# A two-layer hybrid decoder step: the queries' projection beside the selection bits, x kept in DRAM meanwhile, conditioning steps regrouped

## The chip, the cores and the metric

The kernel runs on one NeuronCore of a Trainium2 chip. TensorE (PE) multiplies matrices into PSUM, VectorE (DVE), ScalarE (ACT) and GpSimd (POOL) work elementwise, and SyncE (SP) issues nearly all of the DMAs, one after the other in the order in which they are written. Each engine has its own instruction stream, and semaphores connect the streams. The metric is the device time of one execution in microseconds, lower is better.

## The reference, cut to what matters

One inference step for 1024 new prompt rows and 8 samples of 4 new rows each (1056 rows in all, width 1024). Layer 0 is attention in which an indexer chooses the keys; layer 1 pools over windows; each is followed by an MLP. Every layer is conditioned on a vector c by shifts, scales and gates.

```python
for i in range(DEPTH):                                  # 2 layers
    mod = silu(c) @ w_mod[i] + b_mod[i]                 # 1024 -> 6*1024: the conditioning
    sh1, sc1, g1, sh2, sc2, g2 = jnp.split(mod, 6, axis=-1)
    h = modulate(rmsnorm(x, norm_mix_g[i]), sh1, sc1)
    m = dsa_mixer(h) if i == 0 else pool_mixer(h)
    x = x + g1[:, None, :] * m
    h = modulate(rmsnorm(x, norm_ffn_g[i]), sh2, sc2)
    x = x + g2[:, None, :] * (jnp.square(relu(h @ w_up[i])) @ w_down[i])

# dsa_mixer, layer 0
q, k, v, qi, ki, wi = jnp.split(h @ w_in, PROJ_SPLITS, axis=-1)   # 1024, 256, 256, 512, 64, 8 columns
logits = jnp.einsum('nqhd,nsd->nqhs', qi, kidx) * IDX_DIM ** -0.5
score = jnp.einsum('nqhs,nqh->nqs', relu(logits), wi) * IDX_HEADS ** -0.5
_, idx = lax.top_k(where(causal, score, -inf), k_sel)   # the best 256 (samples: 129) keys of each row
o = softmax attention of q over the chosen k, v         # 8 heads, 2 key heads
return o.reshape(n, t, -1) @ w_o
```

The samples' past keys, values and indexer keys lie in pages of 128 rows, found through page_table.

## The kernel before, in words

Everything is written by hand, engine by engine, in blocks; at the end of a block all engines meet at a barrier. x lies transposed in SBUF for the whole run (128 partitions, 8 chunks of 1056 columns). All large products are made in three parts: weights and rows are split into an upper and a lower half (hhi, hlo for the rows; whi, wlo for the weights), and `products` (L501) runs 24 matmuls of 352 columns for one unit of 128 output columns and a third of the rows. A *unit* of weights comes in three steps: SP loads it (`load_unit`, L463, 512 KB, which waits until the unit before the last has been split), ACT makes whi (`split_unit_hi`, L473), POOL makes wlo (`split_unit_lo`, L479). There are two slots, so the next unit can be made ready while PE multiplies with this one.

A *conditioning step* is 256 of the columns of w_mod: a load of 1 MB (L408), a product with the conditioning vector (`mod_product`, L424, 8 matmuls), a copy of the result by DVE, a fold by PE (`mod_turns`, L433) and an addition of the bias by DVE (`mod_bias`, L439). There are 48; they are placed wherever PE has time.

The blocks that matter here, in order:

- **Load and first norm** (0 to 50 us): x comes in and is transposed, 8 conditioning steps.
- **Projection** (L923, 50 to 263 us): 17 units. Units 0 and 1 give v, 2 and 3 k, 4 to 11 the queries q, 12 the indexer's key and weights, 13 to 16 the indexer's queries. SP's stream holds nothing but the unit loads.
- **Indexer** (L1045, 263 to 369 us): logits and scores, 8 conditioning steps, and the zeroed and regrouped queries of the samples, `qps` (L1250).
- **Selection** (L1305, 369 to 525 us): the threshold of the 256th best score is found bit by bit, in 31 bits. In each, ACT counts four of the seven score tiles against the candidate (L1382) and DVE three (L1445), and DVE sets the bit. Beside the bits run 30 conditioning steps, and the samples' past keys are loaded page by page (`load_kpg`, L395, and `load_pages`, L390), transposed on PE (L1339), copied and multiplied with `qps` (L1352).
- **Samples' attention** (L1533), **prompt attention** (L1676), **output projection** (L1817, x is added to here for the first time, L523), then the MLPs and layer 1.

The page loads need a page number from SBUF each, so SP reads a register before every one:

```python
def load_pages(sp, dst, cache, signal, b):                       # L390
    for n in range(PAGES):
        sp.dma_start(dst[:, n, :], cache[0, bass.ds(page(sp, b, n), 1)]...)
```

Of the kernel before, what the change touches and what calls it, by code (L numbers as in the profile page):

```python
# [16 lines left out]
NB = 8  # L17
# [51 lines left out]
U_KIWI = 12  # L69
# [73 lines left out]
def hybrid_step(nc, x_prompt, x_sample, cache_k, cache_v, cache_kidx, state_pool, page_table, c_prompt, c_sample,  # L143
# [3 lines left out]
    with ctx:  # L147
# [95 lines left out]
        put = region(r1)  # L243
        score = put("score", [P, P * sum(t + 1 for t in IDX_TILES)])
        scs = put("scs", [NS, SL])
        qps = put("qps", [P, NB, KV, HEADS * DT])
        ptb = put("ptb", [1, NB * PAGES], I32)
        tie = put("tie", [P, SEQ])
        tie_run = put("tie_run", [P, SEQ])
        ssm = put("ssm", [P, 2, SL])  # L250
        kpg = put("kpg", [P, 2, PAGES, KW])

        kir = put("kir", [P, 2, PAGES, ID])
# [3 lines left out]
        wsel = put("wsel", [P, 2, NS])  # L257
        qis = put("qis", [ID, NB, IH * DT])
        qit = put("qit", [ID, IH // 2, NS])


        moved = put("moved", [P, 2, IH // 2, P], F32R)
        assert moved.manual_sbuf_range[1] <= s1
# [3 lines left out]
        ki_hi = at("ki_hi", [P, SEQ], F32R, tie.manual_sbuf_range[0])  # L267
        ki_lo = at("ki_lo", [P, SEQ], F32R, tie_run.manual_sbuf_range[0])

        put = region(kpg.manual_sbuf_range[1])  # L270
        kts = put("kts", [P, 2, KV, PAST])
        junk_a = at("junk_a", [P, SEQ], F32, tie.manual_sbuf_range[0])
        junk_v = at("junk_v", [P, SEQ], F32, tie_run.manual_sbuf_range[0])

        mraw1 = [at(f"mraw1_{i}", [P, KT8, 256], F32, t.manual_sbuf_range[0]) for i, t in enumerate((wraw, whi, wlo))]

# [4 lines left out]
        assert kts.manual_sbuf_range[1] <= pts.manual_sbuf_range[1]  # L281

        vpg2 = put("vpg2", [P, 2, PAGES, KW])
        mrow1 = put("mrow1", [P, 2, 256])
        srows = put("srows", [P, 2, KW])
        assert srows.manual_sbuf_range[1] <= s1

        vpg6 = at("vpg6", [P, NB - 2, PAGES, KW], F32, qi.manual_sbuf_range[0])
        assert vpg6.manual_sbuf_range[1] <= wi.manual_sbuf_range[1]
        vpg = [vpg2[:, b] for b in range(2)] + [vpg6[:, b] for b in range(NB - 2)]  # L290

        put = region(ssm.manual_sbuf_range[0])
# [54 lines left out]
        mraw1_in = [sem(f"mraw1_in{i}") for i in range(3)]  # L347
# [63 lines left out]
        M_INDEX, M_SELECT = 8, 30  # L411
        M_REST = 2 * MOD_STEPS - M_FIRST - M_INDEX - M_SELECT

        MOD_SLOT = [n % 2 for n in range(M_INDEX)] + [n % 3 for n in range(M_SELECT + M_REST)]

        def load_mod1(sp, n):

            load_mod_step(sp, M_FIRST + n, mraw1[MOD_SLOT[n]][:, :, :], mraw1_in[MOD_SLOT[n]])

        def mod1_landed(pe, n):  # L420
            pe.wait_ge(mraw1_in[MOD_SLOT[n]], 16 * MOD_SLOT[:n + 1].count(MOD_SLOT[n]))
            return mraw1[MOD_SLOT[n]]
# [363 lines left out]

        NH = M_FIRST
# [134 lines left out]

        with nc.Block() as block:  # L923
            @block.sync
            def _(sp):
                for u in range(2, N_IN):
                    cols = u_in_cols(u)
                    load_unit(sp, u, raw8(u % 2)[:, :, 0:cols.stop - cols.start],
                              dsa_w_in[0, :, cols].rearrange("(k p) c -> p k c", p=P))

# [12 lines left out]
            def _(act):  # L943
# [16 lines left out]

                norm_root(act, 0)
# [5 lines left out]
                for s in range(6):  # L967
                    part(4 + s)
                    rows_of_v(s)
                for u in range(10, N_IN):  # L970
                    part(u)

            @block.gpsimd
            def _(pool):
                for u in range(N_IN):
                    split_unit_lo(pool, u, u % 2)

            @block.tensor
            def _(pe):
# [19 lines left out]
                for u in range(2, N_IN):  # L999
# [8 lines left out]
                    if 3 <= u < 9:  # L1008
                        rows_of_v(u - 3)

            @block.vector
            def _(dve):
# [5 lines left out]
                for u in range(2, N_IN):  # L1018
                    dst = u_in_dst(u, kt, qt, qi)
                    for c in range(NC):  # L1020
# [9 lines left out]
                        ins.then_inc(down_empty, 1)  # L1030

# [11 lines left out]
        assert len(logit_list) == 10 * M_INDEX and 24 < M_SELECT <= BITS and 2 <= M_REST <= 3  # L1043
        last_logit = {t: max(n for n, l in enumerate(logit_list) if l[0] == t) for t in IDX_TILES}
        with nc.Block() as block:  # L1045
            @block.sync
            def _(sp):
# [12 lines left out]
                load_mod1(sp, 0)  # L1060
# [11 lines left out]
                load_mod1(sp, 1)  # L1072
# [4 lines left out]
                loads += [(10 * n - 11, "step", n) for n in range(2, M_INDEX + 2)]  # L1077
                for _, kind, n in sorted(loads):
                    if kind == "pages":
                        load_kir(n)  # L1080
                        if n < 4:
                            load_kpg(sp, n - 2)
                    else:
                        sp.wait_ge(mod_mm, M_FIRST + n - 1)
                        load_mod1(sp, n)
# [13 lines left out]
            def _(pe):  # L1099
# [34 lines left out]
                def mod_half(m, half):  # L1134

                    if half == 0 and m >= 2:
                        pe.wait_ge(mod_done, M_FIRST + m - 1)
                    weights = mod1_landed(pe, m)
                    mod_product(pe, bank(MOD_BANK[m % 2]), weights, range(4 * half, 4 * half + 4))

                def mod_turn(m):
                    pe.wait_ge(mod_row, M_FIRST + m + 1)
# [23 lines left out]
                pe.wait_ge(mod_done, M_FIRST + M_INDEX)  # L1166
# [5 lines left out]
                for a, (lo, hi) in enumerate(((0, PAST), (PAST, SL))):  # L1172
                    for g in range(2):
                        ins = pe.matmul(pair[3][0:NS, a, 0:hi - lo], wsel[:, g, :], ssm[:, g, lo:hi], start=(g == 0),
# [4 lines left out]
            def _(act):  # L1179
# [37 lines left out]
                for g in range(2):  # L1217
                    act.activation(ssm[:, g, 0:PAST], bank(2 + 2 * g), ACT.Relu, scale=SC_IDX)
                    act.activation(ssm[:, g, PAST:SL], bank(3)[:, DT * g:DT * (g + 1)], ACT.Relu,
# [3 lines left out]
            def _(dve):  # L1223
# [26 lines left out]
                dve.memset(qps[:], 0.0).then_inc(qprep, 1)  # L1250
                dve.wait_ge(qprep, 9)
                for g in range(KV):
                    for r in range(GROUP):
                        h = GROUP * g + r
                        ins = dve.tensor_copy(qps[:, :, g, h * DT:(h + 1) * DT],
                                              qt[:, h, SEQ:ROWS].rearrange("p (b t) -> p b t", t=DT))
                    ins.then_inc(qprep, 1)
                dve.wait_ge(krow_wi, TILES)
                for n, (t, h, c) in enumerate(logit_list):
# [12 lines left out]
                    if n % 10 == 9:  # L1272
# [4 lines left out]
                        else:  # L1277
                            dve.wait_ge(mod_t, M_FIRST + m)
                        dve.wait_ge(mod_mm, M_FIRST + m + 1)
                        dve.tensor_copy(krow[:, 0, 0:256],  # L1280
                                        bank(MOD_BANK[m % 2])[:, 0:256]).then_inc(mod_row, 1)
                    if n % 10 == 5 and n > 10:
                        mod_bias(dve, M_FIRST + n // 10 - 1, bank(MOD_BANK[(n // 10 - 1) % 2])[:, 256:512])
# [6 lines left out]
                mod_bias(dve, M_FIRST + M_INDEX - 1, bank(MOD_BANK[(M_INDEX - 1) % 2])[:, 256:512])  # L1290
# [13 lines left out]
        m1 = M_FIRST + M_INDEX  # L1304
        with nc.Block() as block:  # L1305
            @block.sync
            def _(sp):
                load_mod1(sp, M_INDEX + 2)
                for n in range(3, M_SELECT):
                    sp.wait_ge(mod_mm, m1 + n - 2)  # L1310
                    load_mod1(sp, M_INDEX + n)
                    if n % 3 == 0 and n // 3 + 1 < NB:
                        b = n // 3 + 1
                        if b >= 2:
                            sp.wait_ge(kts_t, 2 * b - 2)
                            load_kpg(sp, b)
                    if n % 3 == 1 and n // 3 < NB:
                        load_pages(sp, vpg[n // 3], cache_v, vpg_in[n // 3], n // 3)
                load_pages(sp, vpg[0], cache_v, vpg_in[0], 0)
                for n in range(M_SELECT, M_SELECT + M_REST):  # L1320
                    sp.wait_ge(mod_mm, m1 + n - 2)
                    load_mod1(sp, M_INDEX + n)
# [7 lines left out]

# [1071 lines left out]
```

## Time and profile before

| | us |
|---|---|
| median of 3 runs | 2475.91 (2474.41 to 2481.66) |
| the profiled execution | 2483.4 |
| its span, first to last instruction | 2481.6 |
| PE busy | 2291.1 (92%) |
| DVE busy | 997.4 (40%) |
| ACT busy | 782.4 (32%) |
| mean granted TensorE clock | 0.952 |

PE is busy nearly everywhere. In forty equal slices of 62 us its busy share is `6999886768888999...`, and the granted clock, in tenths of full speed, is `8999886769999999...`: the slices that are not full are the first and those from about 250 to 560 us, which hold the indexer, the selection and the samples' attention. The DMA engines move 310 GB/s in the slice of 434 to 496 us and 35 to 57 GB/s in the projection. A busy time is summed over an engine's instructions; a wait names what released it. In a timeline row the first number is the start in us, the second the extent of the row from its first to its last instruction, and what stands in brackets is the idle time before it.

### The profile page before, as it was taken

To read this page: it belongs to the slowest core of one execution; us is meant where nothing else is said; L and a number is where in the kernel's file an instruction comes from. 1 tells how busy PE (TensorE), PEld (TensorE's weight loads), DVE (VectorE), ACT (ScalarE), POOL (GpSimd) and SP (SyncE) were. 2 spreads that over 40 slices of the span, in tenths; PEclk is the share of its full clock that TensorE was granted. 3 is DMA by queue.
4 is the path that set the end of the run, shared out by engine and by line. 5 is a ranking of instruction groups with operands and counts; after the bars stand their busy time and mean duration, and the time that the engine had idled before them with its cause. 6 is when DMAs were issued, how large, how long until landed. Compare 5 with 4: busy or idle time off the path is not lost. (4 is left out here: it accounts for less than half of the span.)

```text
span 2481.6 us, 37303 instructions
## 1 busy us (share of the span) xinstructions
PE 2291.1 (92%) x13854; PEld 2082.1 (84%) x13854; DVE 997.4 (40%) x2492; ACT 782.4 (32%) x1418; POOL 623.9 (25%) x355
## 2 busy tenths in 40 slices
PE   6999886768888999999999999978999999999997
PEld 4999543334447899999999999977999999999996
DVE  2411468866543543323323323347333323333325
ACT  4210457844453431221122121345121122121123
POOL 4121000005674621211212121413211212122123
PEclk8999886769999999999999999989999999999999
DMA  7112447920001211111111111100111111111111
GB/s 249 35 39 57 135 128 240 310 69 18 1 1 52 78 52 51 43 51 42 51 42 42 51 42 51 53 25 19 52 52 43 49 44 42 51 42 51 42 42 70
DMA packets 207582, 161.66 MB, mean 65 GB/s; under 512 B 12365, under 2 KB 204093, under 8 KB 207477
## 3 DMA queue, kind: packets, MB, share of 16 engines
q1 hardware_dynamic: 206525, 158.84, 20.6%
q0 software_dynamic: 960, 1.57, 0.3%
q8 instruction: 56, 0.92, 0.2%
q14 instruction: 41, 0.34, 0.0%
HBM read 151.53 MB, written 7.31 MB: 64 GB/s over the span
## 5 line engine op out<-in xcount | busy, mean ns | idle before, releaser
L511 PE MATMUL pair<-hhi,whi 128*128 128x352 f32 x2184 | 712.9, 326 | 26.7 <-DVE hlo L712 8.5
L512 PE MATMUL pair<-hlo,whi 128*128 128x352 f32 x2184 | 703.6, 322 | 0.0
L513 PE MATMUL pair<-hhi,wlo 128*128 128x352 f32 x2184 | 703.1, 322 | 0.0
L2022 POOL TENSOR_TENSOR wlo<-wraw,whi 128x1024 fp32r<-128x1024 f32 x127 | 305.0, 2402 | 1144.9 <-ACT whi L1972 1143.7
L511 PE MATMUL pair<-hidh,whi 128*128 128x352 f32 x1536 | 495.4, 323 | 0.0
L512 PE MATMUL pair<-hidl,whi 128*128 128x352 f32 x1536 | 492.7, 321 | 0.0
L513 PE MATMUL pair<-hidh,wlo 128*128 128x352 f32 x1536 | 492.2, 320 | 0.0
L523 DVE SCALAR_TENSOR_TENSOR x<-pair,mod,x 128x352 f32<-128x352 f32 (+1 forms) x432 | 247.4, 573 | 514.7 <-PE pair L513 513.8
L511 PEld LDWEIGHTS pair<-hhi,whi 128*128 128x128 f32 x2184 | 411.0, 188 | 37.5 <-issue 15.8
L512 PEld LDWEIGHTS pair<-hlo,whi 128*128 128x128 f32 x2184 | 412.2, 189 | 0.4
L513 PEld LDWEIGHTS pair<-hhi,wlo 128*128 128x128 f32 x2184 | 411.1, 188 | 0.5
L1972 ACT ACTIVATE whi<-wraw 128x1024 fp32r<-128x1024 f32 x126 | 132.7, 1054 | 609.5 <-PE pair L513 609.5
L2074 DVE TENSOR_TENSOR squ<-relu 128x352 f32<-128x352 f32 x192 | 101.2, 527 | 493.4 <-ACT relu L1980 493.3
L512 PEld LDWEIGHTS pair<-hidl,whi 128*128 128x128 f32 x1536 | 288.5, 188 | 0.0
L511 PEld LDWEIGHTS pair<-hidh,whi 128*128 128x128 f32 x1536 | 288.3, 188 | 0.0
L513 PEld LDWEIGHTS pair<-hidh,wlo 128*128 128x128 f32 x1536 | 287.9, 187 | 0.0
L1980 ACT ACTIVATE relu<-pair 128x352 f32<-128x352 f32 x192 | 89.3, 465 | 470.9 <-PE pair L513 470.9
L1761 POOL TENSOR_SCALAR ss<-ss,small 128x128 f32<-128x128 f32 (+7 forms) x64 | 125.2, 1966 | 288.3 <-DVE small L1768 287.8
L481 POOL TENSOR_TENSOR wlo<-wraw,whi 128x1024 fp32r<-128x1024 f32 x36 | 89.1, 2477 | 217.1 <-ACT whi L477 217.0
L2078 DVE TENSOR_TENSOR hidl<-squ,hidh 128x352 fp32r<-128x352 f32 x192 | 105.1, 547 | 20.0
L1982 ACT ACTIVATE hidh<-relu 128x352 fp32r<-128x352 f32 x192 | 96.2, 501 | 6.1
L428 PE MATMUL pair<-mraw,csil 128*32 128x256 f32 x768 | 65.9, 459 | 32.3 <-DMA mraw<-in_w_mod_dram 20.4
(265 smaller groups left out, 2043.4 us busy)
## 6 DMA issues: line engine op xcount, KB each, us to landing
mraw<-in_w_mod_dram SPq DMA_DIRECT2D x48, 1024.0 KB, 6.4
wraw<-in_w_up_dram SPq DMA_DIRECT2D x64, 512.0 KB, 3.9
wraw<-in_w_down_dram SPq DMA_DIRECT2D x64, 512.0 KB, 3.3
wraw<-in_dsa_w_in_dram SPq DMA_DIRECT2D x16, 512.0 KB, 3.7
wraw<-in_dsa_w_o_dram SPq DMA_DIRECT2D x16, 512.0 KB, 3.9
xrow<-in_x_prompt_dram SPq DMA_DIRECT2D x8, 512.0 KB, 6.3
kpg<-in_cache_k_dram SPq DMA_DIRECT2D x32, 128.0 KB, 2.4
vpg<-in_cache_v_dram SPq DMA_DIRECT2D x32, 128.0 KB, 3.3
```

The source lines that it names most:

```text
L481: pool.tensor_tensor(wlo[:, slot, :], wraw[:, slot, :], whi[:, slot, :], ALU.subtract).then_inc(lo_ready, 1)
L511: pe.matmul(out, a, hi[:, kr, r], start=(n == 0), stop=False)
L512: pe.matmul(out, a, lo[:, kr, r], start=False, stop=False)
L513: last = pe.matmul(out, b, hi[:, kr, r], start=False, stop=(n == len(ks) - 1))
L523: ins = dve.scalar_tensor_tensor(out=xs, in0=ps[:, 0:n], scalar=mod[:, layer, gate + d, 0:1], in1=xs, op0=ALU.mult, op1=ALU.add)
L1761: pool.tensor_scalar(ss[:, n % SR, 0:L], ss[:, n % SR, 0:L], small[:, 12 + n % SR:13 + n % SR], None, ALU.mult).then_inc(prob_done, 1)
L1972: act.activation(whi[:, slot(k), :], wraw[:, slot(k), :], ACT.Copy).then_inc(hi_ready, 1)
L1980: act.activation(relu[:, p % 3, :], up_bank(f, c, first)[:, 0:CW], ACT.Relu).then_inc(up_empty, 1)
L1982: act.activation(hidh[:, f, c * CW:(c + 1) * CW], relu[:, p % 3, :], ACT.Square).then_inc(square_done, 1)
L2022: pool.tensor_tensor(wlo[:, slot(k), :], wraw[:, slot(k), :], whi[:, slot(k), :], ALU.subtract).then_inc(lo_ready, 1)
L2074: dve.tensor_tensor(squ[:, p % 3, :], relu[:, p % 3, :], relu[:, p % 3, :], ALU.mult).then_inc(hid_square, 1)
L2078: dve.tensor_tensor(hidl[:, f, c * CW:(c + 1) * CW], squ[:, p % 3, :], hidh[:, f, c * CW:(c + 1) * CW], ALU.subtract).then_inc(hid_ready, 1)
```

## The change

- The units are renumbered: 0 and 1 v, 2 and 3 k, 4, 5, 7 and 8 the indexer's queries, 6 the indexer's key and weights, 9 to 16 the queries. The projection block makes 0 to 8 (`U_Q = 9`); units 9 to 16 are made in the selection block.
- The normalised rows hhi and hlo must therefore outlive the projection. x is written to DRAM at the start of the projection block (two DMAs issued by ACT, into the outputs y_prompt and y_sample, which hold nothing yet) and read back at the start of the output projection (two DMAs by ACT); its place in SBUF takes the scores and other buffers.
- 12 conditioning steps move from the selection (30, now 18) into the projection, after products 8, 9, 11, 12 and so on. They have three slots of their own there.
- In the selection, PE makes one product of the queries per bit in bits 0 to 17 and six more in bits 18 to 21; DVE copies each out of PSUM one bit later. The samples' keys follow in bits 23 to 30: their loads, which were spread over the bits, come on SP behind the last product, keys and values of a sample in turn. DVE takes half of the copies of transposed keys.
- `qps` is built in bit 22, not in the indexer.

```diff
 # projection: SP
+                for n in range(2):
+                    load_mod1(sp, n)
-                for u in range(2, N_IN):
+                for u in range(2, U_Q):
                     cols = u_in_cols(u)
                     load_unit(sp, u, raw8(u % 2)[:, :, 0:cols.stop - cols.start],
                               dsa_w_in[0, :, cols].rearrange("(k p) c -> p k c", p=P))
+                    for n in range(2 * (u - 1), min(2 * u, M_PROJ)):
+                        if n >= 3:
+                            sp.wait_ge(mod_mm, MP + n - 2)
+                        load_mod1(sp, n)
 # projection: ACT, then PE
+                act.dma_start(y_prompt[0].rearrange("(k p) c -> p k c", p=P), x[:, :, 0:SEQ]).then_inc(x_out, 16)
+                act.dma_start(spill_s, x[:, :, SEQ:ROWS]).then_inc(x_out, 16)
...
+        MOD_AFTER = {8 + n * 3 // 2: n for n in range(M_PROJ)}
+                        n = MOD_AFTER.get(3 * u + c)
+                        if n is not None:
+                            weights = mod1_landed(pe, n)
+                            if n >= 2:
+                                pe.wait_ge(mod_row, MP + n - 1)
+                            mod_product(pe, bank(n % 2), weights)
+                            if n >= 1:
+                                mod_turn(n - 1)
 # selection: SP
+        Q_BIT = list(range(M_SELECT)) + [18, 19, 19, 20, 21, 21]
+        KTS_BIT = Q_BIT[-1] + 2
+                for n in range(M_SELECT):
+                    load_step(n)
+                    if n % 3 == 2 or n == 3:
+                        u = U_Q + 2 + (0 if n == 2 else 1 if n == 3 else n // 3 + 1)
+                        if u < N_IN:
+                            load_q(u)
...
+                sp.wait_ge(down_ready, G_Q + 24)
+                for b in range(NB):
+                    if b >= 2:
+                        sp.wait_ge(kts_t, 2 * b - 2)
+                    load_kpg(sp, b)
+                    load_pages(sp, vpg[b], cache_v, vpg_in[b], b)
 # selection: PE
+                for n in range(BITS):
+                    for p in range(24):
+                        if Q_BIT[p] == n:
+                            product(p)
+                    if n < M_SELECT:
+                        weights = mod1_landed(pe, M_PROJ + M_INDEX + n)
+                        if n >= 2:
+                            pe.wait_ge(mod_row, m1 + n - 1)
+                        mod_product(pe, bank(n % 2), weights)
+                        if n >= 1:
+                            mod_turn(n - 1)
+                for b in range(NB + 1):
+                    sample(b)
 # selection: DVE, in each bit
+                    for p in range(24):
+                        if Q_BIT[p] == n - 1:
...
+                            dve.tensor_copy(qt[:, d, c * CW:(c + 1) * CW],
+                                            bank(2 + p % 4)[:, 0:CW]).then_inc(down_empty, 1)
+                    if n >= KTS_BIT and n - KTS_BIT < NB:
+                        b = n - KTS_BIT
+                        dve.wait_ge(kts_t, 2 * b + 2)
...
+                        dve.tensor_copy(kts[:, b % 2, 1, :], bank(0)).then_inc(kts1_done, 1)
 # output projection: ACT, then DVE before its first addition to x
+                act.dma_start(x[:, :, 0:SEQ], y_prompt[0].rearrange("(k p) c -> p k c", p=P)).then_inc(x_in, 16)
+                act.dma_start(x[:, :, SEQ:ROWS], spill_s).then_inc(x_in, 16)
+                dve.wait_ge(x_in, 32)
```

Three places show how instructions moved. The first is SP's stream in the projection block before (wraw is the raw slot of a unit, ki and wi are the indexer's key and weights, out_dram the stored values v):

```order
L924 UNCONDITIONAL_BRANCH [waits barrier_Pool_Activation_PE_DVE_SP_release]
L468 DMA wraw<-in_dsa_w_in_dram 128x8x128 [waits lo_ready,hi_ready] x10
L468 DMA wraw<-in_dsa_w_in_dram 128x8x72 [waits lo_ready,hi_ready]
L468 DMA wraw<-in_dsa_w_in_dram 128x8x128 [waits lo_ready,hi_ready] x4
L932 DMA ki_73<-ki_73 64x1056 [waits down_empty]
L933 DMA wi<-wi 8x1056
```

The same stretch of SP now (mraw_q is a slot of a conditioning step; mod_mm counts the products of conditioning steps that PE has finished):

```order
L939 UNCONDITIONAL_BRANCH [waits barrier_Pool_Activation_PE_DVE_SP_release]
L416 DMA mraw_q_121<-in_w_mod_dram 128x8x256
L416 DMA mraw_q_122<-in_w_mod_dram 128x8x256
L480 DMA wraw<-in_dsa_w_in_dram 128x8x128 [waits lo_ready,hi_ready]
L416 DMA mraw_q_123<-in_w_mod_dram 128x8x256
L416 DMA mraw_q_121<-in_w_mod_dram 128x8x256 [waits mod_mm]
L480 DMA wraw<-in_dsa_w_in_dram 128x8x128 [waits lo_ready,hi_ready]
L416 DMA mraw_q_122<-in_w_mod_dram 128x8x256 [waits mod_mm]
L416 DMA mraw_q_123<-in_w_mod_dram 128x8x256 [waits mod_mm]
L480 DMA wraw<-in_dsa_w_in_dram 128x8x128 [waits lo_ready,hi_ready]
```

From unit 3 on, each unit's load stands behind loads of steps that wait for mod_mm.

SP's stream in the selection before, at the first page loads (kpg and vpg are pages of keys and values, ptb the page table; a page is four rows):

```order
L408 DMA mraw_0_130<-in_w_mod_dram 128x8x256 [waits mod_mm]
L388 TENSOR_LOAD ptb [waits kts_t]
L388 ISA x2
L392 ISA
L392 DMA kpg<-in_cache_k_dram 128x256
```

SP's stream in the selection now, from the last conditioning steps on:

```order
L416 DMA mraw_i_134<-in_w_mod_dram 128x8x256 [waits mod_mm]
L416 DMA mraw_i_135<-in_w_mod_dram 128x8x256 [waits mod_mm]
L396 TENSOR_LOAD ptb [waits down_ready]
L396 ISA x2
L400 ISA
L400 DMA kpg<-in_cache_k_dram 128x256
```

All 64 page loads (32 of keys, 32 of values) stand in one run behind the wait for down_ready, the end of the last product of the queries; before, they stood in fours between the loads of the steps, some of them already in the indexer.

PE's stream in the selection now, at the end of one bit's product and the start of the next (hhi, hlo, whi, wlo make a product of the queries; mraw_i and mrow a conditioning step):

```order
L525 MATMUL pair<-hhi,wlo 128x352
L440 MATMUL pair<-mraw_i_136,csil 32x256 [waits mod_row,mraw1_in7]
L440 MATMUL pair<-mraw_i_136,csil 32x256 x7
L447 MATMUL pair<-cst,mrow_111 128x9 [waits mod_done,mod_row]
L447 MATMUL pair<-cst,mrow_111 128x9
L523 MATMUL pair<-hhi,whi 128x352 [waits down_empty,lo_ready,hi_ready]
```

Each step's product and the fold of the step before it now stand behind a product of 24 matmuls.

## Rows read from the trace of the kernel before

**Rows 1.** Busy time by stretch: engines (instructions), then granted clock, DMA share, GB/s.

```profile
core 0: us, PE busy (x) PEld busy (x) DVE busy (x) ACT busy (x) POOL busy (x), PEclk, DMA share, GB/s
115.00:206.00 91.00, 91.00 (x577) 90.63 (x576) 12.60 (x24) 10.27 (x13) 17.25 (x9) 1.00 0.17 44
440.00:500.00 60.00, 47.79 (x344) 23.42 (x344) 48.83 (x188) 53.51 (x114) 0.00 (x0) 0.75 0.90 302
763.00:770.00 7.00, 3.92 (x13) 3.95 (x14) 6.46 (x6) 7.00 (x18) 5.03 (x2) 0.52 0.26 76
```

**Rows 2.** Timeline, DVE in the projection: copies out of PSUM, one a product.

```profile
110.91 0.53 DVE L1029 COPY kt<-pair 128x352 f32<-128x352 f32 x1 [3.29 <-PE pair L513]
115.17 0.53 DVE L1029 COPY qt<-pair 128x352 f32<-128x352 f32 x1 [3.74 <-PE pair L513]
118.99 0.52 DVE L1029 COPY qt<-pair 128x352 f32<-128x352 f32 x1 [3.29 <-PE pair L513]
```

**Rows 3.** Timeline, SP's unit loads in the projection.

```profile
55.33 2.68 SPq L468 DMA_DIRECT2D wraw<-in_dsa_w_in_dram  x2
87.71 28.08 SPq L468 DMA_DIRECT2D wraw<-in_dsa_w_in_dram  x4
```

**Rows 4.** Loads of units (L468), then of conditioning steps (L408): time to landing.

```profile
DMA to landing us min/median/max: 3.1/3.9/9.5
...
DMA to landing us min/median/max: 4.9/6.4/10.9
```

**Rows 5.** DMA issues: times issued, KB each, median us to landing.

```profile
kpg<-in_cache_k_dram SPq DMA_DIRECT2D x32, 128.0 KB, 2.4
...
xrow<-in_x_sample_dram SPq DMA_DIRECT2D x1, 128.0 KB, 10.6
```

**Rows 6.** Timeline, ACT and POOL: the two halves of one unit's split.

```profile
99.51 1.06 ACT L477 ACTIVATE whi<-wraw 128x1024 fp32r<-128x1024 f32 x1 [10.22 <-PE pair L513]
...
100.65 2.39 POOL L481 TENSOR_TENSOR wlo<-wraw,whi 128x1024 fp32r<-128x1024 f32 x1 [8.88 <-ACT whi L477]
```

**Rows 7.** Timeline, PE after an idle stretch: matmuls 1 and 14.

```profile
766.08 0.63 PE L511 MATMUL pair<-hhi,whi 128*128 128x352 f32 x1 [5.11 <-DVE hlo L1891]
...
770.03 0.37 PE L512 MATMUL pair<-hlo,whi 128*128 128x352 f32 x1
```

**Rows 8.** Timeline, PE: a conditioning step's product, a fold, the next product.

```profile
497.03 1.03 PE L428 MATMUL pair<-mraw,csil 128*32 128x256 f32 x13
...
498.00 0.61 PE L435 MATMUL pair<-cst,mrow 128*128 128x9 f32 x4
...
498.54 1.07 PE L428 MATMUL pair<-mraw,csil 128*32 128x256 f32 x16
```

**Rows 9.** Timeline, selection: its block's start, ACT's first counts, the loop's end.

```profile
368.80 0.06 DVE L1405 MEMSET cnt<- 128x7 f32 x1 [0.33 <-PEq L1045]
...
380.03 1.15 ACT L1382 ACTIVATE junk_a<-score,cand 128x1024 f32<-128x1024 f32 x1 [17.70 <-DVE cand L1425]
...
498.33 1.15 ACT L1382 ACTIVATE junk_a<-score,cand 128x1024 f32<-128x1024 f32 x1
...
502.38 1.15 ACT L1382 ACTIVATE junk_a<-score,cand 128x1024 f32<-128x1024 f32 x1
...
519.03 0.16 DVE L1437 TENSOR_TENSOR cand<-cand,flip 128x4 int32<-128x4 int32 x1
```

**Rows 10.** Timeline, SP in the selection: page loads and a step's load.

```profile
441.88 3.67 SPq L392 DMA_DIRECT2D kpg<-in_cache_k_dram  x4
445.59 0.43 SPq L408 DMA_DIRECT2D mraw<-in_w_mod_dram  x1
446.78 4.00 SPq L392 DMA_DIRECT2D vpg<-in_cache_v_dram  x4
```

**Rows 11.** Timeline, PE: four transposes of a sample's keys.

```profile
440.03 1.11 PE L1339 MATMUL pair<-cst,kpg 128*128 128x128 f32 x4 [1.15 <-ACT kts L1397]
```

**Rows 12.** Timeline, DVE in the output projection: its first addition to x.

```profile
778.07 1.27 DVE L523 SCALAR_TENSOR_TENSOR x<-pair,mod,x 128x352 f32<-128x352 f32 x2
```

More of the change, by code:

```diff
@@ L68 @@
 U_IN, N_IN = 0, 17
-U_KIWI = 12
+U_Q = 9
+U_KIWI = 6
 U_O = U_IN + N_IN
@@ L280, in hybrid_step @@
         pts = put("pts", [P, 2, PAGES + 1, P])
[L281 to L292, printed above, removed]
+        assert pts.manual_sbuf_range[1] <= s1
+        put = region(r1)
         ss = put("ss", [P, SR, SEQ])
@@ L1017, in _ @@
                                     turn_bank(u, c)[:, 0:CW]).then_inc(down_empty, 1)
-                for u in range(2, N_IN):
+                for u in range(2, U_Q):
                     dst = u_in_dst(u, kt, qt, qi)
@@ L1071, in _ @@
                 load_kir(0)
-                load_mod1(sp, 1)
+                load_mod1(sp, M_PROJ + 1)
                 load_kir(1)
                 loads = [(8 * (b - 1), "pages", b) for b in range(2, NB)]
-                loads += [(10 * n - 11, "step", n) for n in range(2, M_INDEX + 2)]
+                loads += [(10 * n - 11, "step", n) for n in range(2, M_INDEX)]
                 for _, kind, n in sorted(loads):
@@ L1329, in mod_turn, with product @@
                     mod_turns(pe, bank(7), mrow1[:, n % 2, :])
+                def product(p):
+                    u, c = U_Q + p // NC, p % NC
+                    if c == 0:
+                        pe.wait_ge(hi_ready, u + 1)
+                        pe.wait_ge(lo_ready, u + 1)
+                    if p >= 4:
+                        pe.wait_ge(down_empty, G_Q + p - 3)
+                    products(pe, bank(2 + p % 4)[:, 0:CW], u % 2, P, slice(0, P), [(k, k) for k in range(KT8)],
+                             hhi, hlo, c).then_inc(down_ready, 1)
                 def sample(b):
@@ L1425, in _, with queries_of_samples @@
                     dve.memset(cand[:, c], 1 << (BITS - 1)).then_inc(signal, 1)
+                def queries_of_samples():
+                    dve.memset(qps[:], 0.0).then_inc(qprep, 1)
+                    dve.wait_ge(qprep, 9)
+                    dve.wait_ge(down_empty, G_Q + 24)
+                    for g in range(KV):
+                        for r in range(GROUP):
+                            h = GROUP * g + r
+                            ins = dve.tensor_copy(qps[:, :, g, h * DT:(h + 1) * DT],
+                                                  qt[:, h, SEQ:ROWS].rearrange("p (b t) -> p b t", t=DT))
+                        ins.then_inc(qprep, 1)
                 def update(n, c, signal):
```

232 lines of the change are left out of this document (130 added, 102 removed).

## The prediction, made before the change was timed

> **What bounds the kernel now.** I read the busy time by stretch first, then the timeline of each stretch that the change touches. In the projection PE is busy 91.0 of 91.0 us at full clock with the DMA engines 17% used [rows 1]: PE is the bound, and whatever leaves it shortens the run. A product ends every 3.82 us there (copies at 115.17 and 118.99) [rows 2]. SP is never late: it issued units 2 and 3 at 55 us and the next as soon as a slot was free [rows 3], and the split of a unit, 1.06 us on ACT and 2.39 on POOL, lies under the product of another [rows 6]. In the selection ACT is busy 53.5 of 60 us, PE 47.8 at a mean clock of 0.75, the DMA engines 90% at 302 GB/s [rows 1]; an undisturbed bit takes 4.05 us (ACT's counts at 498.33 and 502.38), the loop of 31 bits 139.0 us (380.03 to 519.03), so 4.48 a bit [rows 9].
>
> **Projection, what goes.** 24 products of the queries: 24 x 3.82 = 91.7 us, all on PE's path. The transposes of v, which cost four times 4.26 - 3.82 = 0.44 us, six in all and two of them small (110.91 to 115.17) [rows 2], I take as 1.9 us that will now lie in stalls. -93.6.
>
> **Projection, what comes.** 12 conditioning steps on PE: a product and a fold take 498.54 - 497.03 = 1.51 us at full clock [rows 8], 18.1 in all; five folds (0.44 each) fall into the stalls below. +15.9.
>
> **Projection, the new stalls.** SP's stream decides here. The load of unit 3 now stands behind the load of step 3, which waits until PE has finished step 0, and that stands behind the last product of unit 2. So PE finishes unit 2 and the step, and only then is unit 3 asked for. The same holds for unit 4 (behind step 5, whose slot is free after step 2, which stands behind unit 3's last product), and for units 5, 6 and 7; unit 8 goes out right behind unit 7. Five times PE waits for the chain: signal 0.1, loads of a step and of the unit, ACT 1.06, POOL 2.39, and 0.2 for two more signals. The loads are the unknown. The step's 1 MB goes out first, the unit's 512 KB 0.43 us later. Alone, the fastest unit took 3.1 us and the fastest step 4.9 [rows 4], so 0.5 MB more costs 1.8 and both together 4.9 + 1.8 = 6.7. From below, if the unit lands as if alone, at its median: 0.43 + 3.9 = 4.3. From above, by the medians (6.4, and 6.4 - 3.9 = 2.5 more for half as much again): 8.9. That loads do queue shows in one of 128 KB, which took 10.6 us among the first loads, against 2.4 for a page of the same size [rows 5]. I take 6.7, since the DMA engines are otherwise nearly idle here, which makes the fast ends the nearest. A stall is 0.1 + 6.7 + 1.06 + 2.39 + 0.2 = 10.4 us (8.0 to 12.6).
>
> The Trainium skill, DMA: Bandwidth & Descriptors, section Queues, rings and completion order, says that a DMA engine takes the descriptors of a ring in the order given, and that a completion signal lands only after that engine's earlier writes. By that rule the unit can't overtake the step and the bound from below falls away; without it the five stalls would be 5 x 2.4 = 12 us shorter. The 10.6 us row agrees; the range below keeps both.
>
> After a stall PE starts slowly: after 5.1 us idle, 13 matmuls took 770.03 - 766.08 = 3.95 us [rows 7], where 13/24 of 3.82 is 2.07, and the mean granted clock of that stretch was 0.52, the lower level of 1.2 GHz [rows 1]. That is 1.9 us a restart (none at best). Five stalls: 5 x (10.4 + 1.9) = +61.5.
>
> The projection thus comes to -93.6 + 15.9 + 61.5 = **-16.2 us**. ACT's two new DMAs stand in front of the first norm's square root, two issues of about 0.43: **+1**. The 4.33 MB that they move have 40 us until the first moved wait, and nothing here needs DMA bandwidth.
>
> **Indexer.** Nothing. `qps` leaves it, but DVE waited for ACT there after it; its 1.3 us come back in bit 22.
>
> **Selection, bits 0 to 17.** PE now does per bit a product (3.82) and a step (1.51): 5.33 us at full clock, more than ACT's 4.05 and one third of a 1.06 split, and more than DVE's 4.05 at most plus 0.53 for a copy. So PE is the bound, and being busy all the time I give it full clock, as in the projection [rows 1]. The block starts at 368.8 [rows 9]; unit 9 is split by 372.4; the first product at the lower clock (3.82 + 1.9) ends at 378.1, step 0 at 379.2, the second product at 383.0, step 1 at 384.1, and step 17 at 384.1 + 16 x 5.33 = 469.4. Before, bit 17 stood near 380 + 17 x 4.48 = 456. The loads of the steps are no bound any more: 1.17 MB per 5.33 us is 220 GB/s.
>
> **Selection, bits 18 to 22.** Two folds and six products, 0.9 + 6 x 3.82, end at 493.2. The bits themselves need less.
>
> **Selection, bits 23 to 30.** Here is the second new wait. A page load keeps SP for 1.11 us: 446.78 - 441.88 = 4.90 for four and one step's load, less 0.47 for the step, over 4 [rows 10]. All 64 now start after 493.2, keys and values in turn, and bit 23 + b can't pass before the keys of sample b have landed and been transposed. The last page of the keys of sample 7 is the 60th: 493.2 + 0.8 + 59 x 1.11 = 559.5, landed 2.4 later [rows 5], 561.9; eight transposes at the lower clock 2 x 1.11 = 2.2 [rows 11]; a copy 0.6; the rest of that bit, ACT's second pair of counts and DVE's update, some 2.5 of its 4.05. The loop ends near 567.2 instead of 519.2: **+48 us**. Without the page limit it would end near 493 + 5 + 8 x 4.6 = 535, so the limit is 32 of the 48. What is queued behind SP's page loads is nothing but more of them; who waits is PE's transposes, then ACT and DVE, which stand in the middle of a bit.
>
> The Trainium skill, DMA: Bandwidth & Descriptors, section Latency and other measured facts, gives a register load (tensor_load) a floor of about 600 ns. With 0.34 for the DMA itself that is 0.94 a page, and the loop would end 10 us sooner. The rows say 1.11, and the measurement decides.
>
> **Output projection.** x must be back before DVE's first addition, at 778.07 [rows 12], 16 us after the block's start: 4.33 MB at the 302 GB/s of rows 1 are 14.3 us, plus 2.4 to land. **+2** with ACT's issues (0 to 4).
>
> **Sum.** -16.2 + 1 + 48 + 2 = **+34.8 us**. The profiled execution, 2483.4 us with a span of 2481.6, would become 2518.2; its own excess over the median of 2475.91 is not the change's, so for the median I say 2475.9 + 34.8 = **2511 us**.
>
> **Rivals.**
> *Faster: the stalls hardly exist.* If SP's loads came so early that PE never waited, the projection would give 77.7 us and the total -27: 2449. It decides below 5.3 us a stall (26.7 us for five). For it: PE's own work has gone, and the DMA engines are idle. Against it: the split alone is 3.45 of the 5.3, and no unit landed in under 3.1; SP's order would have to be another one.
> *No change: the page loads don't bind.* Then 32 us go: 2479. It would need pages at half of 1.11 us; the two runs of four shown took 3.67 and 4.00 [rows 10].
> *Much slower: PE stays at the lower clock in the selection.* Each bit would then hold a product of 24 x 0.30 = 7.3 and a step of about 2.8; 18 times 4.8 more is 86, the total near 2600. For it: the mean clock of 0.75 before. Against: that went with waits of PE, and PE will have none there.
> *The change doesn't do what it says*, for instance because PE's folds wait for DVE and the products don't overlap the bits: near 2540.
>
> **How the numbers follow.** The forecast 0.78, pages that don't bind 0.08 (of which 0.05 within the bound and 0.03 a little above it), the faster rival 0.06, the clock 0.05, the last 0.03. About 0.3%, 7.4 us, is what a measurement here can tell from no change. Faster is 0.06; the same is 0.08, the 0.05 and 0.03 at the forecast's lower edge; slower the remaining 0.86. The range: from below, stalls of 8.0 without a slow restart (-21.5) and nothing for the output projection: 2487. From above, stalls of 12.6 (+11), steps that land late in the selection or stretches at the lower clock (+8), and 4 elsewhere: 2534.
>
> **What would show it.** In the projection of the changed kernel five idle stretches of PE of about 10 us, released by POOL's wlo, at units 3 to 7, and a unit's load issued right after each step's end; the queries' products gone. Then bits 5.3 us apart until about bit 17, PE near 100% busy at full clock. Then bits about 8.9 us apart (eight pages), with DVE and PE waiting for kpg. The forecast is wrong if PE's idle time in the projection is under 27 us in all, if bits 23 to 30 pass in under 50 us, or if the granted clock between bits 0 and 17 is near 0.5.

## The result, and the profile after

The changed kernel takes 2510.11 us (median of 4 runs, 2509.27 to 2511.56), the kernel before 2475.16 beside it: a ratio of 1.0139, with a 95% interval of 1.0117 to 1.0162, so +34.9 us, where the prediction said +34.8 and 2511. The profiled execution took 2509.73 us with a span of 2507.9.

Busy time by stretch, the changed kernel (to be read beside [rows 1]), the last line from the first norm:

```profile
core 0: us, PE busy (x) PEld busy (x) DVE busy (x) ACT busy (x) POOL busy (x), PEclk, DMA share, GB/s
100.00:200.00 100.00, 64.91 (x434) 56.13 (x433) 10.92 (x27) 6.48 (x10) 9.37 (x4) 0.81 0.29 93
353.00:440.00 87.00, 87.00 (x678) 74.98 (x679) 77.28 (x248) 61.51 (x125) 11.64 (x5) 0.98 0.71 233
477.00:551.00 74.00, 37.67 (x121) 18.50 (x122) 35.31 (x125) 35.84 (x76) 0.00 (x0) 0.66 0.40 114
...
75.90:84.90 9.00, 8.79 (x45) 8.51 (x44) 8.82 (x20) 3.94 (x7) 0.00 (x0) 0.81 0.00 0
```

In the projection PE, busy all the time before, now idles 35 of 100 us. In the first part of the selection it has not a moment free. In the last part it is half idle again, and so are DVE and ACT: none of the computing engines sets the pace.

The timeline of the changed kernel around one stall in the projection answers to [rows 3, 6, 7] (idle time before the instruction in brackets):

```profile
94.68 0.53 DVE L1068 COPY kt<-pair 128x352 f32<-128x352 f32 x1 [3.77 <-PE pair L525]
...
102.21 1.07 PE L440 MATMUL pair<-mraw_q,csil 128*32 128x256 f32 x16
...
103.34 0.37 SPq L416 DMA_DIRECT2D mraw_q<-in_w_mod_dram  x1
103.81 0.53 SPq L480 DMA_DIRECT2D wraw<-in_dsa_w_in_dram  x1
110.06 1.06 ACT L489 ACTIVATE whi<-wraw 128x1024 fp32r<-128x1024 f32 x1 [22.04 <-DMA wraw<-in_dsa_w_in_dram]
111.19 2.34 POOL L493 TENSOR_TENSOR wlo<-wraw,whi 128x1024 fp32r<-128x1024 f32 x1 [20.70 <-ACT whi L489]
113.63 0.63 PE L523 MATMUL pair<-hhi,whi 128*128 128x352 f32 x1 [9.32 <-issue]
...
117.58 0.49 PE L524 MATMUL pair<-hlo,whi 128*128 128x352 f32 x1
...
120.80 9.70 SPq L416 DMA_DIRECT2D mraw_q<-in_w_mod_dram  x2
130.60 0.53 SPq L480 DMA_DIRECT2D wraw<-in_dsa_w_in_dram  x1
```

This is the predicted chain, link by link. PE ends the step's product at 103.28; 0.06 later SP issues the step's load that waited for it, then the unit's. The split starts 6.7 us after the first issue (6.7 predicted), PE restarts at 113.63: 10.35 us after the end of the step's product (10.4), of which it idles 9.32, since transposes of v fill the rest. All five stalls take 9.8 to 10.4 us. After this one the next 13 matmuls take 3.95 us, as in [rows 7].

The selection of the changed kernel (to be read beside [rows 9, 10]): its start, two ends of a bit six bits apart, the last copy of a query product, page loads, the loop's end.

```profile
349.35 0.06 DVE L1482 MEMSET cnt<- 128x7 f32 x1 [0.33 <-PEq L1093]
...
403.60 0.15 DVE L1525 TENSOR_TENSOR cand<-cand,flip 128x4 int32<-128x4 int32 x1
...
436.43 0.15 DVE L1525 TENSOR_TENSOR cand<-cand,flip 128x4 int32<-128x4 int32 x1
...
476.54 0.53 DVE L1545 COPY qt<-pair 128x352 f32<-128x352 f32 x1 [1.79 <-PE pair L525]
...
477.28 4.04 SPq L400 DMA_DIRECT2D kpg<-in_cache_k_dram  x4
482.08 3.63 SPq L400 DMA_DIRECT2D vpg<-in_cache_v_dram  x4
486.47 3.63 SPq L400 DMA_DIRECT2D kpg<-in_cache_k_dram  x4
...
540.18 3.63 SPq L400 DMA_DIRECT2D kpg<-in_cache_k_dram  x4
...
550.93 0.16 DVE L1525 TENSOR_TENSOR cand<-cand,flip 128x4 int32<-128x4 int32 x1
```

Six bits take 32.83 us, 5.47 each, while PE is the bound. The products end 127.2 us after the block's start. Then four pages leave SP every 4.4 us, and a bit takes two such groups. The waits of that last stretch (total us, times, longest) name the keys:

```profile
ACT junk_a L1447 <- DVE cand L1525: 38.9, 10, 5.6
...
DVE kts L1554 <- PE pair L1403: 37.9, 8, 5.9
PE pair L1403 <- DMA kpg<-in_cache_k_dram: 36.8, 8, 6.7
```

PE waits for keys, DVE for PE's transposes, ACT for DVE. In the output projection the changed kernel's first addition to x [rows 12] comes at

```profile
808.99 1.27 DVE L535 SCALAR_TENSOR_TENSOR x<-pair,mod,x 128x352 f32<-128x352 f32 x2
```

which is 258.1 us after the end of the loop; before, it was 259.0. The table sums this up to that addition, from the two traces:

| stretch | before, us | after, us | difference | predicted |
|---|---|---|---|---|
| start to the last copy of the projection | 261.96 | 249.29 | -12.7 | -15.2 |
| from there to the selection's block | 106.8 | 100.1 | -6.8 | 0 |
| selection's block to the end of the loop | 150.2 | 201.6 | +51.3 | +48 |
| from there to the first addition to x | 259.0 | 258.1 | -1.0 | +2 |
| sum | 778.07 | 808.99 | +30.9 | +34.8 |

Behind that point the program is the same, but the profiled execution of before was 8 us above its median and lost some 4.6 us more there, so the spans differ by 26.3 only. By the medians it is 34.9. The rest of those 8 us, some 3.6, lies somewhere in the upper rows of the column before, so no single difference is good to better than a few us.

### The profile page after: what moved, and what is told of

The parts are those of the page before. It is cut to its first block and busy times, and to the rows that moved or that the text cites. A ratio compares the mean times of both kernels' runs of the same rounds, so it can differ in the third digit from the quotient of the medians.

```text
span 2507.9 us, 37312 instructions
## 1 busy us (share of the span) xinstructions
PE 2283.9 (91%) x13854; PEld 2080.3 (83%) x13854; DVE 1010.0 (40%) x2500; ACT 777.4 (31%) x1410; POOL 622.2 (25%) x355
## 3 DMA queue, kind: packets, MB, share of 16 engines
q0 software_dynamic: 960, 1.57, 0.3%
## 5 line engine op out<-in xcount | busy, mean ns | idle before, releaser
L523 PE MATMUL pair<-hhi,whi 128*128 128x352 f32 x2184 | 721.1, 330 | 62.0 <-issue 23.8
L1863 POOL TENSOR_SCALAR ss<-ss,small 128x128 f32<-128x128 f32 (+7 forms) x64 | 124.4, 1954 | 190.9 <-DVE small L1870 190.6
L1447 ACT ACTIVATE junk_a<-score,cand 128x1024 f32<-128x1024 f32 (+2 forms) x93 | 83.9, 902 | 71.7 <-DVE cand L1525 60.8
```

Source lines behind the costliest of these rows:

```text
L523: pe.matmul(out, a, hi[:, kr, r], start=(n == 0), stop=False)
L1863: pool.tensor_scalar(ss[:, n % SR, 0:L], ss[:, n % SR, 0:L], small[:, 12 + n % SR:13 + n % SR], None, ALU.mult).then_inc(prob_done, 1)
```

## The experiments

All times are medians, beside 2510.1 us of the changed kernel; the kernel before stood at 2474.1 to 2475.2 us beside each of them.

**Units' loads ahead (e1).** Only SP's order in the projection changes (`load_in(u)` is the `load_unit` of unit u):

```diff
-                for u in range(2, U_Q):
-                    load_unit(sp, u, ...)
-                    for n in range(2 * (u - 1), min(2 * u, M_PROJ)):
-                        if n >= 3:
-                            sp.wait_ge(mod_mm, MP + n - 2)
-                        load_mod1(sp, n)
+                load_in(2)
+                load_mod1(sp, 2)
+                load_in(3)
+                load_in(4)
+                for n in range(3, M_PROJ):
+                    sp.wait_ge(mod_mm, MP + n - 2)
+                    load_mod1(sp, n)
+                    if n % 2 == 0 and 3 + n // 2 < U_Q:
+                        load_in(3 + n // 2)
```

> The changed kernel, with SP's loads in the projection in another order: each unit's load is issued one unit earlier, ahead of the conditioning steps' loads that wait for PE. Theory (SP's order makes the five stalls): PE is idle for 45 us between 100 and 250 us of the changed kernel's trace and restarts slowly five times (about 1.9 us each); both go, so the projection ends about 45 to 54 us sooner, the time falls from 2510 to about 2460, and no idle stretch of PE over 3 us is left at units 3 to 8. Rival (the loads or the split are late anyway, because 1.5 MB a unit has to land): the stalls shrink by half at most, 2485 or more.

2455.8 us, 54.4 less, and 0.9914 of before (0.9881 to 0.9947). The projection ends at 193.1 instead of 249.3. By stretch:

```profile
100.00:193.00 93.00, 93.00 (x706) 81.99 (x705) 18.03 (x44) 7.89 (x11) 11.90 (x5) 1.00 0.43 137
```

PE has no idle time left and the full clock. Without the five stalls the projection is 56.2 us shorter. The prediction priced them at 61.5 with their slow restarts, less 4.1 for the folds and transposes that it let lie in them, so 57.4. The stalls came from the order of SP's stream alone.

**Unit before step (e7).** After the same wait, the unit's load is issued first and the step's behind it:

```diff
 ...
+                load_in(2)
+                for n in range(2, M_PROJ):
+                    if n >= 3:
+                        sp.wait_ge(mod_mm, MP + n - 2)
+                    if n % 2:
+                        load_in(3 + n // 2 - 1)
+                    load_mod1(sp, n)
+                load_in(8)
```

> The changed kernel, with one thing swapped in the projection: after the same wait for PE, SP issues the next unit's load first and the conditioning step's load behind it. Theory (loads of a queue are served in the order in which they were given, so the unit waited for the step's 1 MB): the unit lands 3.9 us after its issue instead of 6.1, and is issued 0.47 us sooner; each of the five stalls shrinks by about 2.7 us, the projection ends 13 us sooner, time about 2497. Rival (both loads share the DMA engines evenly, so what comes second slows what came first): only the 0.47 us of issue, 2 to 3 us in all, about 2507.

2500.2 us, 10 less (theory 2497, rival 2507). In its profiled execution, 6 us below that median, the projection ends 14.6 us sooner. In its timeline the split starts 4.4 us after the unit's issue, where it was 6.25:

```profile
102.42 0.37 SPq L480 DMA_DIRECT2D wraw<-in_dsa_w_in_dram  x1
102.84 14.36 SPq L416 DMA_DIRECT2D mraw_q<-in_w_mod_dram  x2
...
106.80 1.06 ACT L489 ACTIVATE whi<-wraw 128x1024 fp32r<-128x1024 f32 x1 [19.84 <-DMA wraw<-in_dsa_w_in_dram]
```

The load that was asked for first landed as if alone (median 4.2 us to landing in this stretch, against 6.1), so the two don't share evenly. The rule of the Trainium skill (DMA: Bandwidth & Descriptors, Queues, rings and completion order) that the prediction weighed, descriptors of a ring in the order given, agrees with that. The prediction's bound from below of 8.0 us a stall belongs to this other order: here the five stalls take 6.8 to 8.0 us.

**A page number read once (e2), and all read ahead (e2b).** In e2 a register serves the page of keys and the page of values. In e2b all 32 registers are filled before the wait for the last product:

```diff
+                rows = [page(sp, b, n) for b in range(NB) for n in range(PAGES)]
                 sp.wait_ge(down_ready, G_Q + 24)
 ...
-                    load_kpg(sp, b)
-                    load_pages(sp, vpg[b], cache_v, vpg_in[b], b)
+                    for n in range(PAGES):
+                        for dst, cache, signal in ((kpg[:, b % 2], cache_k, kpg_in[b % 2]), (vpg[b], cache_v, vpg_in[b])):
+                            sp.dma_start(dst[:, n, :], cache[0, bass.ds(rows[b * PAGES + n], 1)]...
```

> The changed kernel, with each page number read into SP's register once and used for the page of keys and the page of values: 32 register loads instead of 64 in the selection's last bits. Theory (SP's 1.11 us a page, 0.77 of it the register, sets the pace of bits 23 to 30): a sample takes 4 x 0.77 + 8 x 0.34 = 5.8 us instead of 8.9; the loop ends about 20 us sooner (531 instead of 551 after the start of the span), time about 2490. Rival (what paces those bits is the chain inside a bit, PE's transposes, the two copies and the counts): less than 5 us, 2505 to 2510.

> The changed kernel, with all 32 page numbers read into 32 registers of SP before it waits for the last product of the queries, so that only the 64 DMA issues are left behind that wait. Theory: 64 issues of about 0.37 us end some 24 us after the last product; keys no longer pace the bits, which take about 4.8 us each from the first keys on (landed and transposed about 8 us after the last product); the loop ends about 29 us sooner (522 instead of 551), time about 2481. Between: the 8.4 MB of pages take 28 us at the 302 GB/s seen in the selection before, which would just not show. Rival (chain inside a bit): as with one register for two pages, under 5 us.

2495.7 us and 2480.3 us: 14.5 and 29.8 less. The loops took 184.5 and 170.3 us, against 201.6. The page limit was worth 31.3 us, and the prediction had it at 32. SP's stream with one register for two pages:

```profile
476.46 0.34 SPq L1378 DMA_DIRECT2D kpg<-in_cache_k_dram  x1
476.90 0.38 SPq L1378 DMA_DIRECT2D vpg<-in_cache_v_dram  x1
478.04 0.34 SPq L1378 DMA_DIRECT2D kpg<-in_cache_k_dram  x1
...
479.60 0.34 SPq L1378 DMA_DIRECT2D kpg<-in_cache_k_dram  x1
```

and with all registers filled ahead:

```profile
475.49 0.33 SPq L1378 DMA_DIRECT2D kpg<-in_cache_k_dram  x1
475.91 0.38 SPq L1378 DMA_DIRECT2D vpg<-in_cache_v_dram  x1
476.48 0.33 SPq L1378 DMA_DIRECT2D kpg<-in_cache_k_dram  x1
```

A register and two issues take 1.57 us, two issues alone 0.99. So the register costs 0.58 and an issue 0.50, not the 0.77 that e2's expectation took and the 0.34 of the prediction: the bar of 0.34 is followed by a gap. A sample's pages thus take 4 x 1.57 = 6.3 us and not 5.8, which fits the 17 us that e2 brought in the loop where 20 were expected. The Trainium skill (DMA: Bandwidth & Descriptors, Latency and other measured facts) gives a register load a floor of about 600 ns, and the 0.58 agrees; the 0.34 that the prediction added to it was too small.

**Eight page loads back in the indexer (e4).** After each of two groups of index pages, SP loads four pages that nothing reads:

```diff
                         load_kir(n)
+                        if n < 4:
+                            for m in range(PAGES):
+                                ...
+                                sp.dma_start(dst, cache_k[0, bass.ds(page(sp, n - 2, m), 1)]...
```

> The changed kernel, with eight page loads of keys put back into SP's stream in the indexer where the kernel before had them (two groups of four, behind the index pages of samples 2 and 3); they land in unused memory and nothing reads them, the later loads stay. The indexer took 106.0 us before the change and 99.1 after it, which the prediction had at no difference. Theory (the two groups of page loads held up SP's loads of index pages and of the next conditioning step, and PE waited 4.1 us for that step): the indexer gets 5 to 8 us longer again, time about 2516. Rival (it got shorter since the samples' queries are no longer copied there, or by other buffer homes): the indexer stays at 99 us, time 2510.

2515.9 us, 5.8 more. From the last copy of the projection to the selection's block it takes 103.2 us, against 100.1 in the changed kernel and 94.7 to 99.5 in the eight other kernels of this study, whose indexer is that of the changed one. Waits in the indexer, before the change:

```profile
ACT rl L1213 <- PE pair L1164: 34.6, 45, 6.7
...
PE pair L428 <- DMA mraw<-in_w_mod_dram: 4.1, 1, 4.1
```

in the changed kernel:

```profile
ACT rl L1262 <- PE pair L1213: 26.0, 45, 1.7
```

and with the pages put back:

```profile
ACT rl L1270 <- PE pair L1221: 30.8, 46, 4.6
...
PE pair L441 <- DMA mraw_w<-in_w_mod_dram: 2.8, 1, 2.8
```

Both come back with the pages: the longer wait of ACT for PE, and PE's wait for the weights of a step, which the changed kernel doesn't have. In the traces the pages account for 3 of the 7 us beside the changed kernel and for 6 beside the mean of the other eight (97.0); by the medians they cost 5.8. The rest stays open, and so does whether it is SP's time or the pages' transfers that delays the step.

**A third of the product left out (e6).** To e2b is added that the queries' products leave out the low half of the weights:

```diff
-                last = pe.matmul(out, b, hi[:, kr, r], start=False, stop=(n == len(ks) - 1))
+                if not short:
+                    last = pe.matmul(out, b, hi[:, kr, r], start=False, stop=(n == len(ks) - 1))
```

> The changed kernel with the page numbers read ahead, and with the third part of each of the queries' products left out (the low half of the weights; 8 of 24 matmuls, 1.27 us a product, 24 products), so the output is not the reference's. Theory (PE is the bound in bits 0 to 17): a bit falls from 5.45 us to the next limit, the counts of ACT and DVE, 4.05 to 4.5; with bits 18 to 22 that is 18 x 0.95 + 4 = 17 to 25 us off the loop, which then takes 147 to 153 us (150.4 before the change, 170.3 with the page numbers ahead); time 2455 to 2463. Rival (ACT, DVE or the loads of steps and units set 5.45): the bits stay above 5.2, under 5 us gained.

2467.7 us, 12.6 below e2b; the loop takes 159.4 us instead of 170.3. Bits 0 to 17 take 4.92 us each instead of 5.29, and those that no load disturbs 4.05 to 4.4. So PE was the bound, as said. But the gain is two thirds of the least expected, since the steps' loads come next, and PE restarts slowly after such a wait (1.93 us for 16 matmuls that take 1.07, at a granted clock of 0.51):

```profile
382.12 1.93 PE L440 MATMUL pair<-mraw_i,csil 128*32 128x256 f32 x16 [3.22 <-DMA mraw_i<-in_w_mod_dram]
...
389.48 1.07 PE L440 MATMUL pair<-mraw_i,csil 128*32 128x256 f32 x16
```

SP's order has a hand in this wait, too:

```profile
356.40 4.57 SPq L416 DMA_DIRECT2D mraw_i<-in_w_mod_dram  x2
374.21 0.37 SPq L480 DMA_DIRECT2D wraw<-in_dsa_w_in_dram  x1
374.62 4.40 SPq L416 DMA_DIRECT2D mraw_i<-in_w_mod_dram  x3
```

The weights for which PE waits until 382.12 were asked for at 374.62, behind a unit's load for which SP waited until 374.21 (for POOL's wlo, which frees the slot). An order without that wait was not run.

**Both orders mended (e5).** The diffs of e1 and e2b together.

> The changed kernel with both edits of SP's stream that worked alone: the units' loads ahead in the projection (2510 to 2455.8) and the page numbers read ahead in the selection (2510 to 2480.3). Theory (the two waits lie in different stages and don't cover each other): the gains add, 54 + 30, time about 2426, which is 2% faster than the kernel before. Rival (one wait hides part of the other, or a third takes their place, the DMA bandwidth in the last bits for one): 2440 or more.

2421.9 us, 88.3 below the changed kernel and 0.9788 of before (0.9760 to 0.9817). The two gains add (54.4 + 29.8 = 84.2). Before the last bits and in them (columns as in the first fence),

```profile
300.00:380.00 80.00, 80.00 (x649) 67.98 (x648) 69.90 (x227) 61.32 (x127) 9.53 (x4) 1.00 0.69 224
413.00:457.00 44.00, 25.95 (x124) 13.19 (x123) 35.68 (x124) 35.79 (x76) 0.00 (x0) 0.84 0.63 192
```

PE now idles 18 of 44 us, while before them it has no gap.

**Six steps moved into the last bits (e8), and off DVE's path (e9).** On top of e5, six of the 18 steps stand in bits 23 to 28:

```diff
+        STEP_BIT = [3 * (m // 2) + m % 2 for m in range(EARLY_STEPS)] + [KTS_BIT + m for m in range(M_SELECT - EARLY_STEPS)]
 ...
                 for b in range(NB + 1):
                     sample(b)
+                    if EARLY_STEPS + b < M_SELECT:
+                        step(EARLY_STEPS + b)
```

> As the kernel with both orders of SP mended, and six of the 18 conditioning steps of the selection moved from the bits in which PE is the bound to bits 23 to 28, where PE waits; the other 12 stand in two of every three of bits 0 to 17. Theory: 6 x 1.51 = 9 us less on PE's path before the last product, and nothing added behind it: 7 to 10 us faster than the kernel with both orders mended (2417 if that is 2426). Rival (the last bits can't take them: 5 MB more of loads beside 8.4 MB of pages in 41 us is 330 GB/s, over the 302 seen, or the steps' products delay the transposes and with them the counts): the same time or up to 10 us slower.

2436.9 us, 15 slower than e5. The products end 117.2 us after the block's start instead of 126.9, about the 9 us expected; but from there to the loop's end it takes 69.6 us instead of 43.8. Waits there:

```profile
ACT junk_a L1469 <- DVE cand L1547: 33.4, 10, 5.7
DVE mrow L1582 <- PE pair L440: 19.7, 6, 4.3
...
PE pair L1428 <- ACT kts L1491: 15.2, 7, 2.6
```

DVE's copy of a step's row, in the middle of a bit, waits 3.3 us for a product that stands behind the transposes and the sample's product of that bit. In e9 it stands one bit later, and SP asks for the weights of such a step one sample later:

```diff
-[KTS_BIT + m for m in range(M_SELECT - EARLY_STEPS)]
+[KTS_BIT + 1 + m for m in range(M_SELECT - EARLY_STEPS)]
```

> As the kernel with six steps moved into the last bits (2436.9), but VectorE copies the row of such a step one bit later, when it has long been computed, and SP asks for the next step's weights one sample later. What is to be told apart: in that kernel the products of the queries ended 9.8 us sooner, but bits 23 to 30 took 69.6 us instead of 43.8. Theory (VectorE's copy of the step's row, in the middle of a bit, waited 3.3 us a bit for PE, behind the transposes, the samples' products and the step, all of one bit): the copy no longer waits, the last bits fall back to 44 to 50 us, time 2412 to 2418, faster than the 2421.9 of both orders mended. Rival (PE's own time or the 5 MB of extra loads beside the pages hold up the last bits): they stay above 60 us, time above 2428.

2419.0 us (0.9776 of before, 0.9755 to 0.9798). The last bits fall to 51.4 us (44 to 50 expected) and that wait is gone. But keys are late again:

```profile
PE pair L1428 <- DMA kpg<-in_cache_k_dram: 13.7, 6, 5.6
DVE kts L1576 <- PE pair L1428: 12.9, 8, 2.4
```

The steps' loads stand among the pages on SP, and the DMA engines are 76% used at 245 GB/s between 404 and 460, where e5 has 63% and 192 in its last bits; which of the two makes the keys late was not separated. The theory holds in the main: the wait that it named is gone, and with it 18 us of the last bits. But SP's order changed in the same run, and the time was missed by 1 us. Between 2419.0 and 2421.9 these runs can't decide. By the medians both are 2.1 to 2.2% faster than the kernel before; the interval of e5 reaches down to 1.8%, that of e9 to 2.0%.

## Why the prediction was right

The number is right within 1 us, and the two mechanisms that carry it are right; that it is so close is in part luck. By the traces the four rows of the table miss by +2.5, -6.8, +3.3 and -3.0 us, and their sum is 30.9, not 34.8. The medians say 34.9 because the profiled execution of before was slow itself, in a stretch that one trace doesn't name.

- **The stalls.** 9.8 to 10.4 us measured, 10.4 said, with the 6.7 us to the split in the one shown, and the same slow restart. From the first copy of k (94.68, before 91.82) to the last copy, the projection lost 15.5 us where 16.2 was said.
- **The head of the projection.** +1 was said, +2.9 measured. ACT's two issues are 0.9 of it. The rest lies in the first products of the projection. PE had waited 2.35 us for DVE there, went on at full clock, and between 77.1 and 80.5 the granted clock was 0.50; the mean of nine us is 0.81 (last line of the first fence). The same products had full clock in the kernel before (first line) and in e5 (second line), where PE had waited 2.32 us each time. Up to there e5 differs from the changed kernel in SP's order alone:

```profile
75.00:84.00 9.00, 8.79 (x55) 8.50 (x54) 8.85 (x20) 3.96 (x7) 0.00 (x0) 1.00 0.00 0
...
75.90:84.90 9.00, 8.79 (x55) 8.50 (x54) 8.85 (x20) 3.94 (x7) 0.00 (x0) 1.00 0.00 0
```

  So the moved work doesn't force the fall, and in e5 the first copy of k comes at 93.07, +1.25, near the +1 that was said. The other nine traces with the moved work, three of them with e5's order in the projection, show 0.81 to 0.87 in the same nine us. Whether the change makes the fall more likely can't be told from one trace of before.
- **The indexer.** This term was wrong: "Nothing" was -6.8. The prediction looked at DVE's work that left and not at SP's stream, from which eight page loads left as well. e4 brings back 3 to 6 of it.
- **Selection, PE as the bound.** 5.47 us a bit, 5.33 said; the products end 127.2 us after the block's start, 124.4 said. e6 shows that PE's work was the limit. It also shows how near the next one is: the prediction called the steps' loads "no bound any more", and with 1.27 us less on PE a bit they are.
- **Selection, pages.** Products' end to loop's end: 74.4 us, 74.0 said. Without the limit 43.5 (e2b), near the 42 that the prediction allowed for it (493 to 535). The sum of 1.11 a page was right (1.10 by the groups of 4.4 us); the 0.34 for the DMA in it was not.
- **Output projection.** +2 was said; nothing is seen. The later of x's two loads was issued at 792.24 and landed 15.3 us after that, at 807.5, while DVE was busy with other work until the first addition at 808.99.
- **Rivals.** Stalls that hardly exist and pages that don't bind take another order of SP's stream, as e1 and e2b show: 2455.8 against 2449, 2480.3 against 2479. PE at the lower clock in the selection did not happen (0.98 between 353 and 440), and the products do lie beside the bits: PE is busy 87.0 of those 87.0 us.

## What to carry to other kernels

When work moves into a stage, write out the queue that feeds it, line by line, and ask for each load which wait stands ahead of it: here one order of issue cost 54 us, another 30, and with both mended the same move was worth 2% instead of costing 1.4%. A load that needs only a free buffer goes ahead of one that waits for a product, and address registers are filled while the queue has nothing to do. A copy that another engine's late work feeds does not belong inside the loop body that sets the pace.

## What was not expected of the hardware

A DMA that SP shows as 0.33 to 0.38 us long took 0.50 us of its stream, and the register load before it 0.58: the bars alone underrate the queue. PE's restart was the same after 5.1 us without work [rows 7] and after 9.3 (at 113.63): 13 matmuls in 3.95 us at a granted clock of 0.50, the lower level of 1.2 GHz, and from 118.13 on 0.16 us a matmul at full clock.
